# Rwkv chunks: the product with the triangle's inverse in two matmuls a head, and the masks of a chunk's scores made one chunk later

## The reference, cut to what matters

```python
def _rwkv7_step(state, inp):
    r_t, w_t, k_t, v_t, a_t, b_t = inp
    sa = jnp.einsum('bhvk,bhk->bhv', state, a_t)
    state = (state * w_t[:, :, None, :] + sa[..., None] * b_t[:, :, None, :]
             + v_t[..., None] * k_t[:, :, None, :])
    y_t = jnp.einsum('bhvk,bhk->bhv', state, r_t)
    return state, y_t
```

## Time and profile before

| | us |
|---|---|
| median of 3 runs | 1428.59 |
| the profiled execution, its own time | 1430.37 |
| its span, first to last instruction | 1428.6 |
| PE busy | 1403.1 (98%) |
| POOL busy | 756.0 (53%) |
| ACT busy | 655.0 (46%) |
| DVE busy | 639.8 (45%) |

### The profile page before, as it was taken

The page is one execution under the profiler, slowest core; times in us unless marked ns, Lnnn a source line. Parts: engine busy times, 40 slices in busy tenths (PEclk is TensorE's granted clock), DMA queues, the critical chain, the costliest instruction groups (busy, mean ns, idle before and its releaser), DMA issues.

```text
span 1428.6 us, 23720 instructions
## 1 busy us (share of the span) xinstructions
PE 1403.1 (98%) x9324; PEld 1154.3 (81%) x9324; DVE 639.8 (45%) x833; ACT 655.0 (46%) x1134; POOL 756.0 (53%) x600
## 2 busy tenths in 40 slices
PE   9999999999999999999999999999899999999998
PEld 6888888777779888888888887777778878888887
DVE  5566656542245433333454856444355352111222
ACT  6555555544346544444332467455453323222343
POOL 4444443355347666666656546954238545444563
PEclk9999999999999999999999999999999999999999
DMA  5222222231131232322333312200013222223232
GB/s 209 91 87 82 81 75 89 70 107 60 59 133 45 74 103 88 103 90 101 103 103 104 118 45 89 75 19 3 3 61 131 98 95 89 97 95 103 88 102 75
DMA packets 34217, 122.98 MB, mean 86 GB/s; under 512 B 3792, under 2 KB 4304, under 8 KB 34000
## 3 DMA queue, kind: packets, MB, share of 16 engines
q1 hardware_dynamic: 33408, 119.51, 24.7%
q10 hardware_dynamic: 720, 2.20, 0.4%
HBM read 119.59 MB, written 2.10 MB: 85 GB/s over the span
## 4 chain that ended last, share of the span: by engine, by line
PE 91%; DVE 3%; POOL 2%; ACT 2%; issue 1%; DMA 1%; SPq 0%; ACTq 0%; POOLq 0%; DVEq 0%
PE ps L553 19%; PE ps L555 19%; PE ps L554 19%; PE ps L1329 2%; PE ps L1330 2%; PE ps L1331 2%; PE ps L1407 2%; PE ps L1408 2%; PE ps L1406 2%; PE ps L660 1%; PE ps L688 1%; PE ps L675 1%; PE ps L918 1%; PE ps L933 1%; PE ps L934 1%
## 5 line engine op out<-in xcount | busy, mean ns | idle before, releaser
L2062 POOL TENSOR_TENSOR w_lo<-stage,w_hi 128x512 fp32r<-128x512 f32 x422 | 591.2, 1425 | 507.0 <-ACT w_hi L1437 506.8
L553 PE MATMUL ps<-x_hi,w_lo 128*128 128x512 f32 x888 | 350.6, 395 | 0.0
L555 PE MATMUL ps<-x_hi,w_hi 128*128 128x512 f32 x888 | 346.0, 390 | 0.0
L554 PE MATMUL ps<-x_lo,w_hi 128*128 128x512 f32 x888 | 345.8, 389 | 0.0
L1437 ACT ACTIVATE w_hi<-stage 128x512 fp32r<-128x512 f32 x422 | 241.6, 622 | 64.2 <-DMA stage<-w 56.6
L553 PEld LDWEIGHTS ps<-x_hi,w_lo 128*128 128x128 f32 x888 | 166.7, 188 | 36.8 <-issue 1.7
L554 PEld LDWEIGHTS ps<-x_lo,w_hi 128*128 128x128 f32 x888 | 166.8, 188 | 35.2 <-issue 1.7
L555 PEld LDWEIGHTS ps<-x_hi,w_hi 128*128 128x128 f32 x888 | 166.6, 188 | 34.9
L2534 DVE SCALAR_TENSOR_TENSOR conv<-ps,vcol,conv 128x511 f32<-128x511 f32 x44 | 33.0, 749 | 132.3 <-ACT conv L1655 132.3
L1655 ACT ACTIVATE conv<-ps,vcol 128x512 f32<-128x512 f32 x44 | 34.2, 778 | 121.1 <-PE ps L555 120.2
L2869 DVE TENSOR_TENSOR bt<-gates,ps 128x512 f32<-128x512 f32 x24 | 16.3, 679 | 142.3 <-PE ps L1408 142.3
(11 more groups left out here) (467 smaller groups left out, 2844.3 us busy)
## 6 DMA issues: line engine op xcount, KB each, us to landing
stage<-w SPq DMA_DIRECT2D x211, 512.0 KB, 3.3
extra_stage<-w SPq DMA_DIRECT2D x6, 512.0 KB, 4.7
H<-xT SPq DMA_DIRECT2D x4, 512.0 KB, 7.7
mem<-memT SPq DMA_DIRECT2D x2, 512.0 KB, 10.9
pool_n<-pool_count ACTq DMA_DIRECT2D x1, 1024.0 KB, 5.4
outT<-outs SPq DMA_DIRECT2D x4, 256.0 KB, 2.0
outT<-outs SPq DMA_DIRECT2D x2, 384.0 KB, 2.7
w_small<-small ACTq DMA_DIRECT2D x1, 512.0 KB, 5.7
```

The source lines that it names most:

```text
L553: pe.matmul(out, wl, hi(k), start=first, stop=False)
L554: pe.matmul(out, wh, lo(k), start=False, stop=False)
L555: mm = pe.matmul(out, wh, hi(k), start=False, stop=end)
L2062: pool.tensor_tensor(unit_lo(b)[:, cols], unit_stage(b)[:, cols], unit_hi(b)[:, cols].bitcast(F32), ALU.subtract).then_inc(wlo_made, 1)
```

## The change

`sa_product` takes the two matmuls that use the upper half of `rh` together: one matmul with the 64 upper rows of `TF` and all its 128 columns as weights writes both halves of bank 7. The matmul of the bottom right part is as before, and is now the last of the head. The two calls of `triangles` for chunks 1 to 3 move from the end of the chunk before into the chunk itself: the first behind the masks of level 2, the second behind those of level 3. Chunk 0 is as it was.

```diff
@@ -1187,9 +1187,8 @@
                 pe.wait_ge(ch_rh_s, c + 1)
                 for h in range(8):
                     cols = slice(h * HD_A, (h + 1) * HD_A)
-                    pe.matmul(ps[0:HB, 7, cols], TF[0:HB, h, 0:HB], rh[0:HB, cols], start=True, stop=True)
-                    pe.matmul(ps[HB:P, 6, cols], TF[HB:P, h, HB:P], rh[HB:P, cols], start=True, stop=True)
-                    mm = pe.matmul(ps[HB:P, 7, cols], TF[0:HB, h, HB:P], rh[0:HB, cols], start=True, stop=True)
+                    pe.matmul(ps[:, 7, cols], TF[0:HB, h, :], rh[0:HB, cols], start=True, stop=True)
+                    mm = pe.matmul(ps[HB:P, 6, cols], TF[HB:P, h, HB:P], rh[HB:P, cols], start=True, stop=True)
                 mm.then_inc(ch_samm_s, 1)
 
             def state_product(c):
@@ -2197,14 +2196,14 @@
                 for l in range(2, NL + 1):
                     for g in range(2):
                         masked(c, l, g)
+                    if c and l in (2, 3):
+                        triangles(c, l - 2)
                     if c == 0 and l == 4:
                         split_lo(U0["conv"] + 2)
                 if c < NS - 1:
                     for g in range(2):
                         t_first(c + 1, g)
                         masked(c + 1, 1, g)
-                    for q in range(2):
-                        triangles(c + 1, q)
```

## The result

The changed kernel takes 1447.03 us in the median of 4 runs (1446.52 to 1448.18) against 1428.61 us: the ratio is 1.0127 with a 95% interval of 1.0114 to 1.0139, 18.4 us slower. The forecast was slower by 6.2 us, 1434.8, with a range up to 1439.0. The sign was right and the size a third of the real one. The profiled execution has a span of 1446.5 us where the one of before had 1428.6.

A forecast was written before the change was run, and what follows sets the result against it. PE was taken to bound the kernel after the chunks, the order of waits in the chunk loop. Product delays 9.8, last supply gap -1.9 and half clock -1.7 gave +6.2 us, 1434.8 us; range 1429.5 to 1439.0.

The forecast's parts named there:

- Bound and supply: PE's delays after the chunks count in full; its four unexplained gaps of 0.23 to 1.83 us are its program running out.
- The product at full clock: In sa_product, 16 form changes a chunk: 593 ns a head, 4.60 us first to last start, 3.66 us added a chunk.
- Rival B: In sa_product, no drain between different rows: product stays at 0.94 us, 1421.8 to 1423.5 us; chance 0.12.
- rival C: In sa_product, a cheaper drain or partly free form changes: 1.5 to 2.5 us a chunk, 1429 to 1432; chance 0.10.
- Triangles: At chunk boundaries, earlier masks start the product 0.86, 0.09 and 0.2 us sooner; the moved calls, 1.8 us each, cost nothing.
- The clock: At 1026.8 to 1030.2 us, PE's half-clock stretch goes if PE does not stop before it: -1.7 us, bounds -1.7 and +1.7.
- The fourth stall: PE's 1.83 us gap at 1026.48 vanishes, -1.9 us, and the half-clock stretch directly behind it goes too, -1.7 us.
- Rival A: Drain occurs, but the 1026.48 gap or half clock stays or comes elsewhere: +7.9 to +9.8, 1436.5 to 1438.4; chance 0.30.
- 9.8 forecast for the delays: Slower products less earlier masks and absorbed supply gaps, chunks 1 to 4: 2.3, 2.1, 1.7 and 3.66 us, together 9.8.

The follow-up runs named there:

- the last product alone: Against the kernel before: triangles moved, only the last chunk's product alternates wide and small matmuls, chunks 0 to 2 keep three a head; 1435.27 us, ratio 1.0049.
- The streaming product: Against the kernel before: triangles moved, three matmuls a head, four extra 64x64 matmuls of 512 columns ahead of each product; 1435.92 us, ratio 1.0056.
- the sorted kernel: Against the changed kernel: a product's eight wide matmuls come first, then its eight small ones; 1430.25 us, ratio 1.0018 to the kernel before.

## Why the prediction was wrong

**Bound and supply: right.** PE's delays reached the end: the fourth product starts 10.9 us later than before (1046.70 against 1035.84), it is 4.1 us longer, the stretch of 6.8 us at half clock behind its start adds up to 3.4 us (the last two overlap a little), and the span has grown by 17.9. The reading of the gaps as the program's supply bore two forecasts: that the long ones vanish in the changed kernel, and that the move of the triangles alone gives next to nothing there. The latter I worked out only for its run, and it follows from the same rows: a gap with a fixed end takes back what is gained ahead of it.

**The product at full clock: right in sum, in part by luck.** Forecast were 593 ns a head and 4.60 us a product (up to 4.77). Measured are 617 ns and 4.79 us where the clock holds (in the kernel with the last product alone). Two steps were off, one each way, and in part cancel. From the first wide pass to the second it takes 160 ns, not 190: 112, the pace of passes with 128 columns of weights, and 48 for the change. I had 58 and 104, the pace of the small form and the longer first pass of 256 streamed columns. From the second wide pass to the small one it takes 202 ns, not 148, since a 64\*128 record of 64 columns lasts 272 ns and not 218. The rule of the Trainium skill that was weighed (TensorEngine Tiling (Array Packing), Tiling Modes: a change of mode drains the engine) agrees with this at every change of the product too. Rival B (side by side in two forms) and rival C (changes that are partly free) are dead.

**Triangles: right.** No wait for the mask, no lateness at level 3, 1.8 us a call in POOL's slack.

**The clock: this step failed.** In "The fourth stall" the clock stood as -1.7 us, with bounds of -1.7 and +1.7, "if the slower product itself is followed by a half-clock stretch". One such stretch was allowed for; there are four, and three of them of 6.8 us. Rival A had half clock that "stays or comes elsewhere", but priced it at the same 1.7 us, and its upper end was 1438.4. Put together: 9.8 forecast for the delays, 0.8 for the 0.19 us that each product takes longer at full clock, 1.9 off for the fourth gap, gives 8.7 us. Measured are 18.4, so that some 9.7 us are left for the clock, by subtraction. The forecast's miss of 12.2 us is these 9.7, the 1.7 that was not won, and the 0.8. The upper bound from the profile is not far: half of 23.9 us is 12.0, and it costs less since thin work does not slow down in full (a head takes 1013 ns at half clock in place of 617, not 1234). The streaming product gives another measure: between its ratio and the changed kernel's lie 10.1 us, of which 1.8 is the difference of their products' lengths, which leaves 8.3.

I had the rows for it, in a way: I had just worked out that the product would spend most of its 4.6 us on changes of form, four times, and had a stretch at half clock in the same part of the trace. But I took that stretch only as something to be won. That was wrong twice. The runs of the kernel before show it: 42 of the 64 beside the experiments have a mean clock of 1.000, against 0.999 in the profiled one, and on none of the three chips is the median of those at 0.999 more than 0.7 us above that of those at 1.000. So the 1.7 us were not there to win in the median.

**What stays open.** What exactly the chip counts as activity was not tried. Shown is that the clock stays at 1.00 with 3.4 us of streaming in a quarter of the array and falls with alternation of about the same length; that it is the emptying of the array, and not something else of a change of form or simply how little is streamed, is argued. The clock also fell at times with hardly any change of form (once in the profile of the sorted kernel, and behind idle gaps of 1.83 and 1.52 us in those of the kernel before and of the triangles alone). Nor was it tried why a fall lasts 3.4 us at one product and 6.8 at another.

## What to carry to other kernels

Count changes of form, not matmuls: dropping one of three matmuls that ran side by side saved nothing, and the form that differed from its neighbour's cost 3.9 us a product and the clock behind it. Give small matmuls of a group one form, if need be by padding the weights with zeros, or at least sort them by form, which got back most but not all here; and where a stretch of PE's time is made of changes of form, price the half clock with it, whatever its busy share says. Before counting a gain ahead of a gap that ends by nothing the profile shows, ask whether that gap will give it back.

## What the runs showed of the hardware

- A change of form costs 148 ns from the last start of a 64-column 64\*64 matmul to the next matmul's, 202 ns from that of a 64\*128, at every change in the product; the first pass behind it is longer by 49 ns (64\*64, 267 against 218) or 48 ns (64\*128, 320 against 272), and by 104 ns where a 64\*128 streams 256 columns.
- fp32 passes with 64 columns streamed: every 58 ns with 64 columns of weights, every 112 ns with 128, in the 64\*128 and in the 128\*128 form alike; two 64\*128 on different rows run side by side.
- PE's clock fell to half in or right behind each alternating product (in the changed kernel for 6.8, 6.8, 3.4 and 6.8 us), also between dense 128x128 matmuls, while PE shows 100% busy in the rows at half; a streaming product of 4.33 us left it at 1.00. At half clock a head of the product takes 1013 ns in place of 617.
- PE stopped for 0.2 to 1.8 us at places a multiple of 256 of its own records apart, those of its sequencer counted (11406, 12942, 14478 and 15246 in the kernel before, whose differences are 6, 6 and 3 times 256). What makes a block run out is open: blocks that took 3.0 us passed without a stop in the same traces. The Trainium skill (Runtime: NRT & Kernel Launch, Instruction fetch mechanics) has blocks of 256 instructions, which agrees, and their fetching as mostly hidden, which holds in the kernel before at 12 of the 16 block boundaries from the first of these gaps to the last and not at these four. 64 useless records in chunk 0 removed two of the four, cut a third to 0.27 us and made the kernel 2.2 us faster.
